# The delta rule's chunk inverse: one side by products, the other by a 32x32 block transpose on DVE

## The reference, cut to what matters

```
decay = exp(where(incl, g[:, None] - g[None, :], -inf))
m     = where(strict, (k_beta @ k.T) * decay, 0)          # 64x64, strictly lower
t_inv = triangular_solve(eye + m, eye, unit_diagonal)     # (I + m)^-1
u = t_inv @ (v * beta);   w = t_inv @ (k_beta * exp(g))
v_new = u - w @ state
o     = (q * exp(g)) @ state + a_intra @ v_new
state = state * exp(g_last) + k_dec.T @ v_new
```

## Time and profile before

| | us |
|---|---|
| three runs | 2453.39, 2454.69, 2458.83 (median 2454.69) |
| the profiled execution | 2453.89, of which span 2452.1 |
| busy: PE, PEld, DVE, ACT, POOL | 2235.2, 1739.4, 1142.7, 731.6, 373.5 |
| stage `delta_and_window`, first to last step | from 374 to about 824 |

### The profile page before, as it was taken

How to read it: one execution, slowest core, us unless ns; L and a number is a source line. 1 busy time by engine, 2 the same in 40 slices (tenths; PEclk the granted TensorE clock), 3 DMA queues, 4 the chain that set the end, 5 groups by cost and what they waited for, 6 DMA issues and landing times. The chain is left out here.

```text
span 2452.1 us, 36802 instructions
## 1 busy us (share of the span) xinstructions
PE 2235.2 (91%) x15922; PEld 1739.4 (71%) x15950; DVE 1142.7 (47%) x1627; ACT 731.6 (30%) x1263; POOL 373.5 (15%) x305
## 2 busy tenths in 40 slices
PE   3999997899999799999957788799999999999998
PEld 2888885677777577877834345477878878878877
DVE  3574323555545576223139366646342442442343
ACT  3222312233323235111131366535221221221221
POOL 3000002222223454000014132144000000000000
PEclk9999996799989799999978799999999999999999
DMA  3213322000000464445210400222111112112112
GB/s 128 93 43 88 92 78 82 1 2 2 2 2 2 181 197 153 128 156 172 86 47 2 186 1 1 87 81 66 52 41 54 43 36 59 44 43 61 43 35 85
DMA packets 185221, 169.13 MB, mean 69 GB/s; under 512 B 13449, under 2 KB 163805, under 8 KB 184933
## 3 DMA queue, kind: packets, MB, share of 16 engines
q1 hardware_dynamic: 179006, 146.74, 19.2%
q0 software_dynamic: 5360, 19.92, 2.1%
q10 hardware_dynamic: 694, 0.13, 0.0%
HBM read 138.46 MB, written 28.31 MB: 68 GB/s over the span
## 5 line engine op out<-in xcount | busy, mean ns | idle before, releaser
L244 PE MATMUL mix_acc<-mix_hi,w_hi 128*128 128x512 f32 x1040 | 410.6, 395 | 6.1 <-DVE w_lo L232 6.1
L246 PE MATMUL mix_acc<-mix_hi,w_lo 128*128 128x512 f32 x1040 | 409.4, 394 | 0.0
L245 PE MATMUL mix_acc<-m_lo,w_hi 128*128 128x512 f32 x1040 | 409.3, 394 | 0.0
L227 ACT ACTIVATE w_hi<-w_stage 128x1024 fp32r<-128x1024 f32 x160 | 169.0, 1056 | 612.8 <-PE mix_acc L246 259.0
L232 DVE TENSOR_TENSOR w_lo<-w_stage,w_hi 128x1024 fp32r<-128x1024 f32 x160 | 201.2, 1258 | 230.5 <-ACT w_hi L227 230.5
L2749 DVE SCALAR_TENSOR_TENSOR hidden<-mix_acc,hidden_conv,hidden 128x1023 f32<-128x1023 f32 x88 | 112.8, 1282 | 263.5 <-ACT hidden L2708 262.0
L244 PEld LDWEIGHTS mix_acc<-mix_hi,w_hi 128*128 128x128 f32 x1040 | 195.7, 188 | 54.6 <-DVE w_lo L232 10.0
L246 PEld LDWEIGHTS mix_acc<-mix_hi,w_lo 128*128 128x128 f32 x1040 | 195.7, 188 | 44.9
L245 PEld LDWEIGHTS mix_acc<-m_lo,w_hi 128*128 128x128 f32 x1040 | 195.7, 188 | 44.7
L244 PE MATMUL acc<-h_hi,w_hi 128*128 128x512 f32 x432 | 171.0, 396 | 4.8 <-DVE h_lo L629 4.8
L246 PE MATMUL acc<-h_hi,w_lo 128*128 128x512 f32 x432 | 169.2, 392 | 0.0
(11 more groups left out here) (314 smaller groups left out, 3647.4 us busy)
## 6 DMA issues: line engine op xcount, KB each, us to landing
w_stage<-in_w_in SPq DMA_DIRECT2D x48, 512.0 KB, 5.4
w_ada<-in_w_ada SPq DMA_DIRECT2D x48, 512.0 KB, 5.0
w_stage<-in_w_up SPq DMA_DIRECT2D x44, 512.0 KB, 3.8
w_stage<-in_w_out SPq DMA_DIRECT2D x32, 512.0 KB, 4.0
spill<-y_tok POOLq DMA_DIRECT2D x24, 512.0 KB, 4.5
m_resid<-resid_spill SPq DMA_DIRECT2D x2, 4096.0 KB, 14.2
conv_in<-spill SPq DMA_DIRECT2D x3, 2048.0 KB, 12.4
w_stage<-in_w_down SPq DMA_DIRECT2D x16, 384.0 KB, 3.4
```

What stands on the lines that cost most here:

```text
L227: nc.scalar.activation(w_hi[:, slot], w_stage[:, slot], ACT.Copy).then_inc(w_hi_ready, 1)
L244: nc.tensor.matmul(acc[:, h, :], w_hi[:, slot, k, :], hi[:, k, tok], start=k == 0, stop=False)
L245: nc.tensor.matmul(acc[:, h, :], w_hi[:, slot, k, :], lo[:, k, tok], start=False, stop=False)
L246: mm = nc.tensor.matmul(acc[:, h, :], w_lo[:, slot, k, :], hi[:, k, tok], start=False, stop=k == kts - 1)
```

## The change

PE's products for kind 0 go, except in the last level. After every addition to kind 1, one DVE instruction, `nc.vector.transpose` (STREAM_TRANSPOSE in the order), writes kind 0. It turns each 32x32 block in place. Up to level 4 the inverse is zero outside the 32x32 blocks on its diagonal, so turning the blocks turns the whole. The last level still forms, for each half, only the kind used later.

Level 0 loses both its PE groups and `corner_mask`: inside blocks of two, the transposed inverse is the unit matrix minus one entry of m, so `first_inverse` multiplies `pair_keys` by a new constant mask, adds the unit matrix, and transposes. It stands ahead of `subtract_state`. `out_add` moves from the end of the step up to just behind the last level's `inv_add`, ahead of the window work of gap (5, 1).

```diff
+    first = np.zeros((P, CH), f)
+    first[p[i64 % 2 == 0], i64[i64 % 2 == 0] + 1] = -1.0
...
+        SUMS, STORED = LEVELS - 1, 2 * LEVELS - 1
...
                 def corner_sum(n, lv):
-                    if lv == 0:
-                        pe.wait_ge(s_scores, n + 1)
-                    else:
-                        pe.wait_ge(s_xu, LEVELS * n + lv)
+
+                    pe.wait_ge(s_xu, STORED * n + 2 * lv)
...
                 def inv_sum(n, lv):
 
                     pe.wait_ge(s_ym, LEVELS * n + lv + 1)
-                    for kind in range(2):
-                        if lv == 0 and kind == 0:
-                            continue
-                        for h in range(DN_HEADS):
-                            for hf in range(2):
-                                if lv == LEVELS - 1 and kind != kind_of(n, hf):
-                                    continue
...
+                    for h in range(DN_HEADS):
+                        for hf in range(2):
+                            r = rows_of(hf)
+                            y, t_old = corner[r, lv, h, :], inv[r, n % 2, 1, h, :]
+                            kind = kind_of(n, hf) if lv == LEVELS - 1 else 1
+                            first = P + (kind * DN_HEADS + h) * LOWER
+                            mm = nc.tensor.matmul(tri[r, first:first + LOWER], y if kind else t_old,
+                                                  upper(t_old, lv) if kind else lower(y, lv), start=True, stop=True)
                     mm.then_inc(s_xs, 1)
...
                     for lv in range(LEVELS):
-                        if s < NCH:
+                        if s < NCH and lv:
                             corner_sum(s, lv)
...
+                def turn_inverse(n, lv):
+
+                    dve.wait_ge(s_xu, STORED * n + 2 * lv + 1)
+                    nc.vector.transpose(inv_flat(n, 0), inv_flat(n, 1)).then_inc(s_xu, 1)
+
+                def first_inverse(n):
+
+                    dve.wait_ge(s_scores, n + 1)
+                    nc.vector.tensor_tensor(corner[:, 0], pair_keys[:, n % 3, :, 1, :],
+                                            first_pairs.unsqueeze(1).to_broadcast([P, DN_HEADS, CH]), ALU.mult
+                                            ).then_inc(s_ym, 1)
+                    if n >= 2:
+                        dve.wait_ge(s_vsum, n - 1)
+                    dve.wait_ge(s_ym, LEVELS * n + 1)
+                    nc.vector.tensor_tensor(inv[:, n % 2, 1], corner[:, 0],
+                                            unit.unsqueeze(1).to_broadcast([P, DN_HEADS, CH]), ALU.add).then_inc(s_xu, 1)
+                    turn_inverse(n, 0)
+
                 def inv_add(n, lv):
...
+                    if lv < LEVELS - 1:
+                        dst = upper(inv_flat(n, 1), lv)
+                        nc.vector.tensor_tensor(dst, tri[:, 2 * P:3 * P].rearrange("p (m c) -> p m c", c=b), dst, ALU.add
+                                                ).then_inc(s_xu, 1)
+                        turn_inverse(n, lv)
+                        return
...
                 for s in range(NCH + 1):
+                    if s < NCH:
+                        first_inverse(s)
                     if s:
                         subtract_state(s - 1)
                     for lv in range(LEVELS):
-                        if s < NCH:
+                        if s < NCH and lv:
                             corner_mask(s, lv)
...
                         if s and lv == 4:
                             advance(s - 1, 0)
+                        if s and lv == 5:
+                            out_add(s - 1)
                         in_gap(s, lv, 1)
-                    if s:
-                        out_add(s - 1)
                     if s + 1 < NCH:
                         scores_of(s + 1)
```

More of the change, by code:

```diff
@@ L89, in shape_constants @@
         "dn": {"reset": reset},
-        "step": {"join": join, "unit": one_unit},
+        "step": {"join": join, "unit": one_unit, "first": first},
         "sums": {"sums": sums},
@@ L772, in build @@
         parts = const("parts").rearrange("p (r c) -> p r c", r=8)
-        unit = const("unit")
+        unit, first_pairs = const("unit"), const("first")
         beta, k_scale, g_exp, g_neg = (scales[:, :, 0], scales[:, :, 2], scales[:, :, 3], token_args[:, :, 4])
@@ L861, in inv_flat @@
             return inv[:, n % 2, kind].rearrange("p h c -> p (h c)")
[L863 to L868, removed]
         def kind_of(n, hf):
@@ L988, in gram @@
                     if n:
-                        pe.wait_ge(s_xu, LEVELS * n)
+                        pe.wait_ge(s_xu, STORED * n)
                     for h in range(DN_HEADS):
@@ L1005, in corner_sum @@
                             r = rows_of(hf)
-                            old = inv[r, n % 2, 0, h, :] if lv else unit[r]
                             mm = nc.tensor.matmul(tri[r, h * LOWER:(h + 1) * LOWER], pair_keys[r, n % 3, h, 1, :],
-                                                  lower(old, lv), start=True, stop=True)
+                                                  lower(inv[r, n % 2, 0, h, :], lv), start=True, stop=True)
                     mm.then_inc(s_y, 1)
@@ L1048, in v_sum @@
                     pe.wait_ge(s_vr, n + 1)
-                    pe.wait_ge(s_xu, LEVELS * (n + 1))
+                    pe.wait_ge(s_xu, STORED * (n + 1))
                     pe.wait_ge(s_pair, min(n + 2, NCH))
@@ L1304, in corner_mask @@
                     b = 1 << lv
-                    dve.wait_ge(s_y, LEVELS * n + lv + 1)
+                    dve.wait_ge(s_y, SUMS * n + lv)
                     summed = tri[:, 0:DN_HEADS * LOWER].rearrange("p (h m c) -> p h m c", h=DN_HEADS, c=b)
@@ L1312, in inv_add @@
                 def inv_add(n, lv):
                     b = 1 << lv
[L1314 to L1320, removed]
+                    dve.wait_ge(s_xs, SUMS * n + lv)
@@ new lines, in inv_add @@
+                    if lv < LEVELS - 1:
[4 more added lines that the diff above has]
+                        return
+                    for hf in range(2):
+                        r, kind = rows_of(hf), kind_of(n, hf)
+                        dst = halves(inv_flat(n, kind)[r], lv)[:, :, kind, :]
+                        first = P + kind * DN_HEADS * LOWER
@@ L1321, in inv_add @@
                         ins = nc.vector.tensor_tensor(
-                            inv[:, n % 2, 1], tri[:, 2 * P:4 * P].rearrange("p (h c) -> p h c", h=DN_HEADS), whole,
+                            dst, tri[r, first:first + DN_HEADS * LOWER].rearrange("p (m c) -> p m c", c=b), dst,
                             ALU.add)
[L1324 to L1337, removed]
```

## The result

The changed kernel takes 2443.99 us (median of 11 runs, 2433.93 to 2452.04) against 2454.17 for the kernel before (11 runs): ratio 0.9945, interval 0.9931 to 0.9959, 10 us less where I had forecast 38. The sign was right; the time lies above the range of 2402 to 2437, and the gain is about a quarter of the forecast.

The account below looks back on a forecast made before the run. PE, nearly full in windowed steps, was taken as the bound except where it waits for DVE. Savings of 23.1 us in eleven steps, plus those in steps 0, 1, 2, 12 and 15, made 38.6: 2416 us, range 2402 to 2437.

Parts of the forecast that it names:

- the sum: Whole kernel: savings in steps 0 to 15 added up to 38.6 us, taking 2453.9 to about 2416.
- a windowed step: Step with window work at full clock: 2.1 us saved, 1.45 at its start and 0.65 in its levels.
- the 2.45 in two steps: Levels 1 to 4: 0.49 us saved in 5 of 8 levels over two steps, where PE's work hides the transpose.
- my take-off of 1.15: Levels 1 to 4, two steps: 1.15 us subtracted where transposes push back the window's maxima or copies; 0.65 a step left.
- The two starts: From gram to level 1's first group: step 7 from 6.19 to about 5.1 us, step 8 from 6.39 to about 4.5.
- The other sign: Sign expected in the new trace: a bare level stays at 2.65 to 2.7 us, as before.
- It is hidden: Start of a step: first_inverse's three DVE instructions, 2.0 us, run beside PE's state sums and two window pieces.
- rival A: Windowed steps: the clock takes the gain back, slower than before; eight slow steps of twelve give 2498. Chance 0.07.
- my slow steps: Windowed steps at the lower clock: 32.2 us instead of 22.0, so each further one costs 10.2.
- rivals B: Windowed steps: one or two further slow ones add 10 to 20 us, giving 2426 to 2436. Chance 0.14.
- Rival C: Step 12 keeps the full clock: 10.2 us more gained, 2406. Chance 0.17.
- the sign of the clock: Behind step 1: more than two steps with PEclk below 0.9 would show the forecast wrong on the clock.

Follow-up runs that it names:

- e4: The kernel before with only out_add moved ahead of the window work of gap (5, 1): 2446.94 us, ratio 0.9970.
- e6: The changed kernel with level 0 by products as before, keeping the transposes in levels 1 to 4 and the moved out_add: 2411.37 us, ratio 0.9819.
- e3: The changed kernel with POOL's store held back until first_inverse of the next step, plus idle matmuls in level 1: 2408.01 us, ratio 0.9811.
- e1: The changed kernel with POOL's store and the scaling behind it held back until first_inverse of the next step is done: 2420.34 us, ratio 0.9858.
- e2: The changed kernel with idle matmuls for PE added in level 1 of steps 3 to 15: 2433.99 us, ratio 0.9907.
- e5: The changed kernel without transposes, levels 1 to 4 forming both kinds by products again, first_inverse and moved out_add kept: 2504.94 us, ratio 1.0197.

## Why the prediction was wrong

- **The step that failed: the sum has no term for the clock.** It adds up what the chain gives and puts further falls at nothing. Without them it was near: eleven steps were to give 23.1 us and step 12 4.5; with the clock taken out steps 3 to 14 gave 27. The 58 us more at half clock took back 26 of that, and 38 less 26 is 12, near the 10 that were measured.
- **The size of a windowed step was right, its make-up less so.** Forecast 2.1 us a step; measured 1.8 in the three steps at full clock, and 2.0 to 2.3 with the clock taken out of all. `out_add` gave 0.7 (forecast 0.9). The transposes gave 1.2 (e4 to e6, 23.6 to 22.4) where I had 0.65: that is the 2.45 in two steps without my take-off of 1.15 for DVE instructions pushed back. Level 0, for which I counted 0.5 to 0.6 a step, gave 0.4. (The two starts, 6.19 to 5.1 and 6.39 to 4.5, average 1.5, not 1.45.)
- **A level.** The transpose cost 0.445, my term 0.42 and 0.03. At half clock a bare level of step 0 went from 3.90 to 3.40 (L1319 at 384.69 and 388.09), forecast 0.44 less. The other sign, a level at full clock of 2.65 to 2.7, came out at 2.58 in e3 (L1325 at 762.62 and 765.20). The rule against more DVE instructions (the Trainium skill, "VectorE: DVE Perf Modes", "Rules for kernel authors") didn't decide here: e6 has 64 more of them than e4, for 1024 matmul records fewer, and is 36 us faster. The estimate of 0.44 from the same page's 311 ns ("The three transpose paths") agrees with the trace.

```profile
384.69 0.29 DVE L1319 TENSOR_TENSOR inv<-tri,inv 128x128 f32<-128x128 f32 x1 [1.17 <-PE tri L1013]
...
388.09 0.29 DVE L1319 TENSOR_TENSOR inv<-tri,inv 128x128 f32<-128x128 f32 x1 [1.17 <-PE tri L1013]
```

- **"It is hidden" failed.** `first_inverse` took 2.8 us in step 4 (505.56 to 508.32), not 2.0. I had moved `out_add` forward and with it POOL's burst, and had moved two instructions with both operands in SBUF right into it, but priced them by the mean of L1319, which in the kernel before took from 0.42 to 1.26. And I asked only whether PE's work covers the three instructions, not what is queued behind them: `subtract_state`, the maxima, then the mask that PE waits for.
- **Why I left the clock out: my argument against rival A**, that PE's busy share of a step hardly falls. It holds (19.62 of 22.06 in step 3) and is beside the point: the falls came behind single thin places. One of the two I had named, the new idle time between the turns; the other, level 1 waiting for its mask behind the maxima, I had not. I priced a fall about rightly (10.2 for 26.5 us at half clock, 0.38 for each; measured 0.39 to 0.47). There were falls in eight steps more than before, but six of the nine lasted 7 us or less, so the loss of 26 us comes to some two and a half of my slow steps: between rivals B (one or two) and A (four and more), where no rival stood and which the range left out.
- **Rival C** (step 12 keeps its clock) didn't come; step 12 fell again, 29.41 us at 0.71. Step 1, for which I had 1.5 less, took 2.0 more.
- **The trace after** answered what I had named: L1013 has 1280 records, transposes 80; no step over 23 us at full clock; PE no longer idle ahead of the state sums; more than two steps below 0.9 behind step 1 (2, 5, 7, 10, 12, 13), which I had put down as the sign of the clock.

The Trainium skill's page "TensorE: Matmul & The Clock Gate", section "Why this matters for your kernels", warns of long idle gaps. Here the rows show falls behind waits of 1.12 and 0.88 us, and of 1.24 and 0.74, with short groups between them, so the gaps don't have to be long ones.

## What to carry to other kernels

When work is taken off an engine that is nearly full, ask where its new idle time lies. Read the emptiest few microseconds of a step, not its mean; if an emptier stretch arises, put falls of the clock there into the sum, with a range, since not every such stretch brings one. Work that is taken away can also have been what filled another unit's wait, as level 0 did between the window's turns. And when instructions are moved, look at what the other engines do at the new place, at the operands they share, and at the whole queue behind the moved work: one wait on POOL, which stood idle for 17.99 us ahead of its store in the changed kernel, was worth more here than the change.

## What the runs showed of the hardware that I had not expected

- A DVE instruction with both operands in SBUF slows beside a POOL tensor instruction: 0.42 alone, 1.10 and 1.08 beside it in step 4 and up to 1.33 elsewhere (L1304 and L1310, 256 elements per partition; e1 against the changed kernel). The block transpose doesn't: 0.445 to 0.446 in all 80, the one at 507.87 beside POOL's L914 included.
- Useless matmuls can make a kernel faster (e2, by 10 us), by holding the clock.
- Two stretches that are equally thin for PE can end with and without a fall (steps 4 and 11 of the changed kernel, 2.18 and 2.11 of 4 us).
- The runs of these kernels scatter differently: 2434 to 2452 over 11 of the changed one, 2405 to 2414 over five of e3, but 2437 to 2462 over 12 of e4, whose profiled run has little time at half clock. Why isn't shown.
- Why slow stretches are longer in e5, where PE has more to do, isn't settled.
